# Extra tokens' factors mostly in PSUM, their activations by ScalarE's queue, first gathers over four tiles, four activation tiles kept in SBUF

## The reference

```python
def _peer(x, w_query, sub_keys, w_down, w_up):
    ...
    sc = jnp.einsum('thpk,hpnk->thpn', q, sub_keys).astype(jnp.float32)
    va, ia = lax.top_k(sc[:, :, 0], PEER_TOPK)
    vb, ib = lax.top_k(sc[:, :, 1], PEER_TOPK)
    cand = (va[..., :, None] + vb[..., None, :]).reshape(n_tok, PEER_HEADS, PEER_TOPK * PEER_TOPK)
    top, flat = lax.top_k(cand, PEER_TOPK)
    expert = ...
    gate = jax.nn.softmax(top, axis=-1).astype(x.dtype)
    ...
        act = _gelu(jnp.einsum('tkd,td->tk', w_down[eb], xb))
        return jnp.einsum('tk,tkd->td', gb * act, w_up[eb])
```

## Time and profile before

| | before |
|---|---|
| median of 3 runs | 1552.93 us (1551.73 to 1554.8) |
| the profiled execution | 1554.64 us, span 1552.5 us |
| mean granted TensorE clock | 0.995 of full speed |
| TensorE busy | 1525.8 us, 98% of the span |
| VectorE busy | 1164.9 us, 75% |
| ScalarE busy | 639.5 us, 41% |
| GpSimd busy | 764.4 us, 49% |
| bytes moved | 419.80 MB, mean 270 GB/s |

### The profile page before, as it was taken

The page is one execution under the profiler, slowest core; times in us unless marked ns, Lnnn a source line. Parts: engine busy times, 40 slices in busy tenths (PEclk is TensorE's granted clock), DMA queues, the critical chain, the costliest instruction groups (busy, mean ns, idle before and its releaser), DMA issues. The chain is left out here.

```text
span 1552.5 us, 23597 instructions
## 1 busy us (share of the span) xinstructions
PE 1525.8 (98%) x8620; PEld 1372.7 (88%) x8620; DVE 1164.9 (75%) x2398; ACT 639.5 (41%) x852; POOL 764.4 (49%) x469
## 2 busy tenths in 40 slices
PE   9999999999999999999999999999999999999997
PEld 8888899889899999999999998988888888888885
DVE  5564262477999978877887875888888888888796
ACT  5323244423234456446644653443333333333333
POOL 2543472224356977878778878632232223323230
PEclk9999999999999999999999999999999999999998
DMA  8532250332246988999899989999999999999991
GB/s 315 182 108 82 95 177 28 108 132 100 81 142 207 349 310 301 356 415 337 304 380 415 314 277 364 327 358 349 345 348 345 354 338 345 347 352 349 372 350 57
DMA packets 146972, 419.80 MB, mean 270 GB/s; under 512 B 18080, under 2 KB 53168, under 8 KB 146352
## 3 DMA queue, kind: packets, MB, share of 16 engines
q1 hardware_dynamic: 101504, 254.42, 46.9%
q0 software_dynamic: 39168, 142.62, 24.8%
q10 hardware_dynamic: 6192, 21.32, 3.5%
HBM read 372.15 MB, written 46.15 MB: 269 GB/s over the span
## 5 line engine op out<-in xcount | busy, mean ns | idle before, releaser
L1578 ACT ACTIVATE w_hi<-raw 128x1024 fp32r<-128x1024 f32 x252 | 266.5, 1058 | 341.6 <-PE ps L1747 299.0
L1317 PE MATMUL ps<-b_hi,w_hi 128*128 128x368 f32 x1024 | 342.1, 334 | 4.3 <-ACT act_t L1584 2.2
L1318 PE MATMUL ps<-b_lo,w_hi 128*128 128x368 f32 x1024 | 337.4, 329 | 0.0
L1319 PE MATMUL ps<-b_hi,w_lo 128*128 128x368 f32 x1024 | 337.1, 329 | 0.0
L1539 POOL TENSOR_TENSOR w_lo<-raw,w_hi 128x1024 fp32r<-128x1024 f32 x119 | 287.2, 2414 | 77.6 <-ACT w_hi L1578 76.4
L1552 POOL DMA_INDIRECT rows<-in_w_up,expert x128 | 152.0, 1188 | 342.0 <-DVE ps L1862 328.9
L1746 PE MATMUL ps<-w_lo,b_hi 128*128 128x512 f32 x768 | 298.8, 389 | 0.0
L1745 PE MATMUL ps<-w_hi,b_hi 128*128 128x512 f32 x768 | 298.8, 389 | 0.0
L1747 PE MATMUL ps<-w_hi,b_lo 128*128 128x512 f32 x768 | 298.8, 389 | 0.0
L1787 DVE SCALAR_TENSOR_TENSOR rows<-rows,ps 128x1024 f32<-128x1024 f32 x128 | 155.4, 1219 | 85.9 <-DMA rows<-in_w_down,expert 80.7
L1869 DVE TENSOR_TENSOR w_lo<-raw,w_hi 128x1024 fp32r<-128x1024 f32 x133 | 162.8, 1224 | 71.8 <-ACT w_hi L1578 71.8
(11 more groups left out here) (284 smaller groups left out, 2544.5 us busy)
## 6 DMA issues: line engine op xcount, KB each, us to landing
raw<-in_down_t SPq DMA_DIRECT2D x128, 512.0 KB, 5.0
raw<-in_up_t SPq DMA_DIRECT2D x128, 512.0 KB, 5.6
raw<-in_units SPq DMA_DIRECT2D x75, 512.0 KB, 3.3
act_d<-act_t SPq DMA_DIRECT2D x128, 192.0 KB, 5.6
c<-act_d SPq DMA_DIRECT2D x128, 192.0 KB, 5.7
gate_d<-gmat ACTq DMA_DIRECT2D x32, 512.0 KB, 8.1
v<-gate_d SPq DMA_DIRECT2D x16, 512.0 KB, 7.3
i<-gate_d SPq DMA_DIRECT2D x16, 512.0 KB, 7.3
```

The lines of the kernel that those rows point to most:

```text
L1317: nc.tensor.matmul(out, ring.w_hi[:, s, w], b_hi[:, c, 0:T], start=c == 0, stop=False)
L1318: nc.tensor.matmul(out, ring.w_hi[:, s, w], b_lo[:, c, 0:T], start=False, stop=False)
L1319: last = nc.tensor.matmul(out, ring.w_lo[:, s, w], b_hi[:, c, 0:T], start=False, stop=c == KC - 1)
L1578: nc.scalar.activation(w_hi[:, u % W4, :], raw[:, u % W4, :], ACT.Copy).then_inc(hi_done, 1)
```

## The change

- The sixteen products of the extra rows, one instruction of 1024 elements each, become three, by a table `X_CHUNKS`: 512 elements against PSUM bank 2, 256 against the upper half of PSUM bank 5, 256 against SBUF as before. ScalarE copies the first four chunks of the tokens' rows to bank 2 at tile 92 (`COPY_TILE`), DVE two more chunks to bank 5 before the first of these dots. Each dot leaves three partial sums; DVE adds them after the last one, and `x_summed` tells ScalarE.
- ScalarE takes the extra dots' Gelu at tile 108 instead of 109, and itself issues the store (in the same step, behind a wait for its own Gelu) and the load back (one step later, behind a wait for the store). SyncE issues neither.
- The intermediate values of `extra_parts` stand in PSUM bank 2 instead of SBUF; `COEF_TILE` goes from 113 to 112, `X_ROUND_TILES` from (116, 119) to (114, 117), `PRODUCT_TILE` from 121 to 119.
- The first four gathers are issued at tiles 11, 12, 13 and 14 instead of all at 11.
- Activation tiles 124 to 127 (`HELD` = 124) are neither stored nor loaded: `product`, `h_high` and `low` take them from `act_t`, after a wait for the Gelu.

```diff
--- before.py
+++ after.py
@@ -1284,6 +1284,7 @@
 ROUNDS = P // RT
+HELD = TILES - ACTS
@@ -1298,9 +1299,11 @@
 NR = HK + XM
-ASK_TILE, DOT_TILE, COEF_TILE = 90, 109, 113
-X_ROUND_TILES = (116, 119)
-PRODUCT_TILE = 121
+X_BANK = 2
+X_CHUNKS = ((0, 4), (4, 6), (6, 8))
+ASK_TILE, COPY_TILE, DOT_TILE, COEF_TILE = 90, 92, 108, 112
+X_ROUND_TILES = (114, 117)
+PRODUCT_TILE = 119
@@ -1387,9 +1390,11 @@
         coef = gparts[:, 0].rearrange("p h k -> p (h k)")
-        x_expert, x_dots, x_coef = sb("x_expert", [P, XM], U32), sb("x_dots", [P, XM]), sb("x_coef", [P, 3, XT])
+        x_expert, x_dots, x_coef = sb("x_expert", [P, XM], U32), sb("x_dots", [P, 3, XM]), sb("x_coef", [P, 2, XT])
...
         x_rows = b_lo[:, :, DT:].bitcast(F32)
+        x_by = (ps[:, X_BANK, :].rearrange("p (c j) -> p c j", j=P),
+                ps[:, PICK_BANK, 2 * P:].rearrange("p (c j) -> p c j", j=P), x_rows[:, 6:8, :])
@@ -1411,6 +1416,9 @@
             return [slice(0, HALF), slice(HALF, D)] if i == TB - 1 else [slice(0, D)]
+
+        def h_part(j):
+            return (h_t[:, j % HS, :] if j < HELD else act_t[:, j % ACTS, :]).rearrange("p (b j) -> p b j", b=DB)
@@ -1434,6 +1442,7 @@
         x_picked, x_ids_stored, x_ids_full = sem("x_picked"), sem("x_ids_stored"), sem("x_ids_full")
+        x_copied, x_summed = sem("x_copied"), sem("x_summed")
@@ -1451,7 +1460,7 @@
-        gathers = [asked(dots[m - ROWS]) if m >= ROWS else LEAD for m in range(NR)]
+        gathers = [asked(dots[m - ROWS]) if m >= ROWS else LEAD + m for m in range(NR)]
@@ -1491,14 +1500,8 @@
                     sp.dma_start(x_expert[:], t["x_ids_d"].rearrange("t (q m) -> q t m", q=XQ)).then_inc(x_ids_full, 16)
-                if u == DOT_TILE + 1:
-                    sp.wait_ge(x_gelu, 1)
-                    sp.dma_start(t["x_act_d"].rearrange("t (q m) -> q t m", q=XQ), x_dots[:]).then_inc(x_act_stored, 16)
-                if u == DOT_TILE + 2:
-                    sp.wait_ge(x_act_stored, 16)
-                    sp.dma_start(x_coef[:, 0], t["x_act_d"].rearrange("t k -> k t"),
-                                 allow_slow_non_contiguous=True).then_inc(x_act_full, 16)
-                sp.dma_start(t["act_d"][u], act_t[:, u % ACTS, :]).then_inc(act_stored[u % ACTS], 16)
+                if u < HELD:
+                    sp.dma_start(t["act_d"][u], act_t[:, u % ACTS, :]).then_inc(act_stored[u % ACTS], 16)
@@ -1512,7 +1515,8 @@
                 load(TILES + j + 2 * W4)
-                load_act(j + 2 * W4)
+                if j + 2 * W4 < HELD:
+                    load_act(j + 2 * W4)
@@ -1607,8 +1611,7 @@
                     act.wait_ge(tile_done, TILES + max(0, j - W4 + 1))
-                nc.scalar.activation(h_slot(b_hi, j % W4), h_t[:, j % HS, :].rearrange("p (b j) -> p b j", b=DB),
-                                     ACT.Copy).then_inc(h_hi_done, 1)
+                nc.scalar.activation(h_slot(b_hi, j % W4), h_part(j), ACT.Copy).then_inc(h_hi_done, 1)
@@ -1628,9 +1631,18 @@
                     gate_out(b, i - CHOICE_TILES)
+                if u == COPY_TILE:
+                    act.wait_ge(x_rows_full, 16 * XQ)
+                    nc.scalar.activation(x_by[0], x_rows[:, 0:4, :], ACT.Copy).then_inc(x_copied, 1)
                 if u == DOT_TILE:
-                    act.wait_ge(row_free, X_FIRST + XM)
-                    nc.scalar.activation(x_dots[:], x_dots[:], ACT.Gelu).then_inc(x_gelu, 1)
+                    act.wait_ge(x_summed, 1)
+                    nc.scalar.activation(x_dots[:, 0], x_dots[:, 0], ACT.Gelu).then_inc(x_gelu, 1)
+                    act.wait_ge(x_gelu, 1)
+                    act.dma_start(t["x_act_d"].rearrange("t (q m) -> q t m", q=XQ), x_dots[:, 0]).then_inc(x_act_stored, 16)
+                if u == DOT_TILE + 1:
+                    act.wait_ge(x_act_stored, 16)
+                    act.dma_start(x_coef[:, 0], t["x_act_d"].rearrange("t k -> k t"),
+                                  allow_slow_non_contiguous=True).then_inc(x_act_full, 16)
@@ -1777,31 +1789,46 @@
                 if x is None:
-                    row, by, m = rows[:, j, :].rearrange("p (i c) -> p i c", i=2), xb, gathered_row(r)
-                    into = dn[:, m:m + 1]
-                else:
-                    if x == 0:
-                        dve.wait_ge(x_rows_full, 16 * XQ)
-                    row, by = rows[:, j, :].rearrange("p (c j) -> p c j", c=KC), x_rows
-                    into = x_dots[:, x:x + 1]
-                nc.vector.scalar_tensor_tensor(out=row, in0=row, scalar=1.0, in1=by, op0=ALU.mult, op1=ALU.mult,
-                                               accum_out=into).then_inc(row_free, 1)
+                    row, m = rows[:, j, :].rearrange("p (i c) -> p i c", i=2), gathered_row(r)
+                    nc.vector.scalar_tensor_tensor(out=row, in0=row, scalar=1.0, in1=xb, op0=ALU.mult, op1=ALU.mult,
+                                                   accum_out=dn[:, m:m + 1]).then_inc(row_free, 1)
+                    return
+                if x == 0:
+                    dve.wait_ge(x_rows_full, 16 * XQ)
+                    step(nc.vector.tensor_copy(x_by[1], x_rows[:, 4:6, :]))
+                    done()
+                    dve.wait_ge(x_copied, 1)
+                for i, (c0_, c1_) in enumerate(X_CHUNKS):
+                    row = rows[:, j, :].rearrange("p (c j) -> p c j", c=KC)[:, c0_:c1_, :]
+                    product_of = nc.vector.scalar_tensor_tensor(out=row, in0=row, scalar=1.0, in1=x_by[i], op0=ALU.mult,
+                                                                op1=ALU.mult, accum_out=x_dots[:, i, x:x + 1])
+                    if i < 2:
+                        step(product_of)
+                    else:
+                        product_of.then_inc(row_free, 1)
+                if x == XM - 1:
+                    done()
+                    dve.wait_ge(row_free, r + 1)
+                    step(nc.vector.tensor_tensor(x_dots[:, 0], x_dots[:, 0], x_dots[:, 1], ALU.add))
+                    done()
+                    nc.vector.tensor_tensor(x_dots[:, 0], x_dots[:, 0], x_dots[:, 2], ALU.add).then_inc(x_summed, 1)
...
-                c, left, part = x_coef[:, 0], x_coef[:, 1], x_part
+                part = x_part
+                whole, left = (ps[:, X_BANK, i * XT:(i + 1) * XT] for i in range(2))
                 tok = slice(XS, P)
-                step(nc.vector.tensor_copy(left, cols[:, 2, tok]))
-                done()
-                step(nc.vector.tensor_tensor(left, left, cols[:, 3, tok], ALU.add))
+                step(nc.vector.tensor_copy(x_coef[:, 1], cols[:, 2, tok]))
+                done()
+                step(nc.vector.tensor_tensor(left, x_coef[:, 1], cols[:, 3, tok], ALU.add))
...
                 done()
-                step(nc.vector.scalar_tensor_tensor(out=x_coef[:, 2], in0=left, scalar=1.0 / GSCALE, in1=c,
+                step(nc.vector.scalar_tensor_tensor(out=whole, in0=left, scalar=1.0 / GSCALE, in1=x_coef[:, 0],
...
                 done()
-                step(nc.vector.tensor_copy(part[:, 0], x_coef[:, 2]))
-                done()
-                step(nc.vector.tensor_tensor(left, x_coef[:, 2], part[:, 0], ALU.subtract))
+                step(nc.vector.tensor_copy(part[:, 0], whole))
+                done()
+                step(nc.vector.tensor_tensor(left, whole, part[:, 0], ALU.subtract))
@@ -1835,9 +1862,12 @@
                 s, g = j % HS, j // GG
-                dve.wait_ge(act_full[s], 16 * (j // HS) + 16)
+                if j < HELD:
+                    dve.wait_ge(act_full[s], 16 * (j // HS) + 16)
+                else:
+                    dve.wait_ge(gelu_done, j + 1)
                 dve.wait_ge(gate_full[g % 2], 16 * (g // 2) + 16)
-                of = h_t[:, s, :].rearrange("p (b j) -> p b j", b=DB)
+                of = h_part(j)
@@ -1846,8 +1876,8 @@
                 dve.wait_ge(h_hi_done, j + 1)
-                nc.vector.tensor_tensor(h_slot(b_lo, j % W4), h_t[:, j % HS, :].rearrange("p (b j) -> p b j", b=DB),
-                                        h_slot(b_hi, j % W4).bitcast(F32), ALU.subtract).then_inc(h_split, 1)
+                nc.vector.tensor_tensor(h_slot(b_lo, j % W4), h_part(j), h_slot(b_hi, j % W4).bitcast(F32), ALU.subtract
+                                        ).then_inc(h_split, 1)
```

## The result

The changed kernel takes **1561.01 us** (median of 7 executions, 1557.87 to 1562.71), the kernel before on the same chip 1553.56 (7 executions, 1551.73 to 1556.07): ratio **1.0046, 95% interval 1.0034 to 1.0058**, so 5.3 to 9.0 us slower. I had forecast 1547.0, in a range of 1542 to 1552. On a second chip it was 1562.13 against 1553.58, ratio 1.0049 (1.0029 to 1.0068).

The account below looks back on a forecast made before the run. TensorE's work plus its gaps was taken as the bound, with only down-stage gaps reachable. Terms -1.3 - 1.5 - 0.3 - 2.7 = -5.8 us took 1554.64 to 1548.8; the median's 1.7 us offset gave 1547.0, range 1542 to 1552.

Parts of the forecast that it names:

- at nothing: Costed at zero: late first gathers 1 to 3, ScalarE's tile 92 copy, held activation tiles, products at tile 119.
- 1.9 unheld or 3.66: DVE's three 16-bit products before the first extra round: 1.9 us undisturbed, or 3.66 us as in the kernel before.
- First gathers: Spreading the first four gathers over four tiles starts POOL's split earlier, ending TensorE's wait near 501 us: -1.3 us.
- Gap 1: TensorE's wait of 1.31 us at 501.02 for POOL's low part of a weight tile, forecast to close.
- A new wait near TensorE's first gate rounds: Sign that the forecast is wrong: TensorE waits there because of the late first gathers; no size given.
- The extra dots: Sixteen DVE dots, each in three pieces, wait less for POOL's splits, shortening a gate-round wait near 900 us: -1.5 us.
- W: Summed waits of the sixteen third (SBUF) pieces for POOL's splits; DVE gains if under 8.4 us.
- rival (c): Slower: third pieces land inside POOL's splits and each waits 1.2 us; +4.8 us, 1557.7 us, chance 0.10.
- gap 2: TensorE's gate-round wait for DVE, 2.54 us at 900.62 plus 1.7 us of half clock; forecast to shrink to 1.9.
- POOL beside the dots: Shorter third pieces hold POOL's gathers less, halving a TensorE wait on POOL's low part at 947.00: -0.3 us.
- gap 3: TensorE's wait of 0.69 us at 947.00 for POOL's low part; half of it forecast to go.
- The way through memory and the extra rounds: Earlier store and load on ScalarE's queue and faster casts cut waits before the extra rounds, 4.0 to 1.3: -2.7 us.

Follow-up runs that it names:

- the fastest version: Kernel before plus three-piece dots (second product's SBUF piece first), intermediates in PSUM, held activation tiles, and extra Gelu, store and load one tile earlier: 1545.31 us, ratio 0.9958.

## Why the prediction was wrong

Three steps failed: the late first gathers, costed "at nothing"; the end of the third pieces, taken from one execution and as random; and the room before the first extra round, with the products at "1.9 unheld or 3.66". (The sum itself has a slip: 1548.8 less 1.7 is 1547.1, not 1547.0.)

**First gathers, -1.3: wrong.** Gap 1 closed as forecast. The step that failed is the lateness "at nothing": I had followed the gathers into DVE's dots, and not POOL's splits into DVE's other work. Two casts and some small steps, all from SBUF to SBUF, had run in the time the four gathers kept free of splits. The picks were 8.2 us later for it, where 5.1 were to spare. By the run of this part alone the term is +3.7 us (+0.5 to +7.1) and not -1.3. "A new wait near TensorE's first gate rounds" stood among the signs of error; I had blamed the gathers for it, and it was the splits.

**The extra dots, -1.5 (ends -4.2 and +9.1): the durations right, the mechanism of the end not.** A 512-piece took 0.69 us and a third 0.42, as worked out. W was 11.1 us in one execution and 3.0 in the other, round the threshold of 8.4, and neither the random arrival nor rival (c) describes it: in the cycle the arrivals are in step with the splits, and in the first execution one row decided it, at about 889 us. Alone the term was -3.9 us (-6.7 to -0.9), which takes in the -1.5; but gap 2, from which I had worked it out, is absent from the profiles of three runs with the old dots, so an agreement would be luck. In the changed kernel the pieces were worth nothing that can be measured (1.0045 without them); with the second piece first the ratio was 1.0022. Rival (c), to which I gave 0.10, had the direction, and its 1557.7 us is nearer than my forecast by luck: it put all of the loss in the pieces, at W = 14.5, while W stayed at 11.1 and of the 7.7 us between the two spans 2.8 stand at the gate rounds.

**POOL beside the dots, -0.3:** no gather beside the dots took over 1.2 us (1.76 before), and gap 3 is in neither profile of the changed kernel. It is also absent from the run with one dot again, so that the shorter gathers closed it is not shown.

**The way through memory and the extra rounds, -2.7: wrong, +1.6 to +2.0.** The store on ScalarE's queue landed after 8.45 us, at the slow end of what I had allowed. The load took 11.3 us where I had carried over 3.71 from SyncE's queue, so it did not land before DVE asked: DVE waited 2.37 us. The wait of ScalarE's Gelu behind the store was 5.08 us and reached TensorE hardly at all. The larger failing term is the products: I took "1.9 unheld or 3.66" for three that took 5.14 and 5.02 us in the two executions and 4.4 to 7.3 in most other runs, although has 5.72 us for the second round's. With 5.14 the gap of "0.2 to 2.0 us" becomes 3.4, and the half clock behind it comes on top. The products are the term that stays when the load is in time (6.47 us, wait 5.0). I had moved the round forward by two tiles and DVE's start by one dot, which takes the room from 9.4 us to 4.6, against 2.9 us gained on the cast and 2.45 on the wait for the load.

**At nothing:** no profile shows a wait that the copies or the held tiles caused. The held tiles with the intermediates in PSUM gave 3.9 us alone (0.9 to 6.8). The casts went from 3.08 to 0.17 us as forecast, but the wait behind them fell by 0.5 us only, as the products took 5.90 us in that run.

**Settled and open.** The wait for the picks comes with the spread gathers and goes with them, in both kernels. The cycle goes when the pieces are undone or put in the other order, and stands in the kernel before with pieces, intermediates and Gelu at 108. The tiles bring the wait of 5 us at the first extra round in the fastest version; in the changed kernel, taking them back only moved it. The sizes are not sharp: the kernel before spans 1547 to 1563 us over its executions, and the parts don't add up. Parts alone: +3.7, -3.9, +3.1, -3.9; sum -1.0; together +7.1. The cycle is the interaction I can show, in profiles; how many of the other executions have it is not shown, only guessed from their times. Why the intermediates and held tiles with the old order of pieces fall into it more often than the pieces alone is open, as is why the changed kernel with SyncE's queue had the worst median of all in six executions.

## What to carry to other kernels

Where an operation keeps two others apart in time, ask what used the gap: follow not only what the moved instruction feeds, but what now runs beside the work that takes its place, on every engine that the rows show held by it. Where one engine's instruction fills half of a loop's period (2.4 of 5.0 us here) and holds another's, the two can stay in step with each other; a profile of one execution then says little, of the kernel before as of the changed one, and the cheap remedy here was to change the order inside the loop, not to shorten the piece. When a round is asked for earlier, count the room between it and the step that prepares it, with the preparation at its longest measured length.

## What was not expected of the hardware

- DVE steps with one input (cast 128x256, SBUF to SBUF) waited out POOL's split just as two-input products do: 3.33 us for 0.28. Casts that read PSUM took 0.17 us beside any split. Copies from SBUF into PSUM were not held either: one of 128x256 elements took 0.43 us at 872.68 with a split running from 872.62 to 875.03 (the run with the tiles alone in the fastest version), and four of the same size in the kernel before took 0.42 us inside splits.
- The same 8 KB load of the coefficients landed after 3.7 to 5.7 us on SyncE's queue (10 runs) and after 6.0 to 18.6 us on ScalarE's (8 runs).
- TensorE's clock, mean of the 3.4 us behind it, was 0.50 to 0.57 after ten waits of 3.4 us and more, and 0.65 after one of 3.65 us. After waits of 2.3 to 3.3 us it fell in some executions (0.50 after 2.7 and 2.8, 0.67 after 2.5) and not in others (1.00 after 2.3, 2.8 and 3.3; after the wait of 3.1 for the picks 0.56 to 0.66 in four executions, 1.00 in four). After the waits of 1.75 us of the changed kernel it did not fall.
- One program on one chip had executions 9 us apart (1554.9 to 1563.7, the changed kernel). In the two that were profiled, on two chips, the cycle begins or not by 0.2 us: one SBUF piece starts 0.03 us after a split or 0.18 us before it, behind a row of a gather. No run moves that row alone.
